# Five weight units instead of four on the first token tile at two stage changes of a two-block transformer kernel

## Chip, cores and metric

The kernel runs on one core of one Trainium2 chip. The metric is the device time of one launch in microseconds (us), lower is better; a figure without a word beside it is the median of several launches on one chip.

## What is computed

The reference is two transformer blocks in a row on one sequence of 256 tokens with model width 1024, in float32. The part that matters here is the second block:

```python
u = rms_norm(x, ffn1_norm_g) * (1 + sc1) + sh1
x = x + 0.5 * g1 * swiglu(u, ffn1_w_in, ffn1_w_out)        # D_FF_2 = 2816
u = rms_norm(x, mix_norm_g) * (1 + sc2) + sh2
z = u @ w_mix + b_mix                                      # then mLSTM and forgetting attention
...
merged = sigmoid(g_a) * (y_a @ w_branch_a) + sigmoid(g_b) * (y_b @ w_branch_b)
x = x + g2 * (merged @ w_out)
u = rms_norm(x, ffn2_norm_g) * (1 + sc3) + sh3
x = x + 0.5 * g3 * swiglu(u, ffn2_w_in, ffn2_w_out)
```

Each `rms_norm` needs the whole row of the new x, and each product after it needs the normed row: these are the points at which the chain of matmuls could break.

## The kernel before

**Units and halves.** All large products stream their weights from HBM in units: two blocks of 128 rows by 512 columns, 512 KB. The units are numbered in the order in which they are used (0 to the end). A unit's life has four steps, on four engines:

- SyncE starts its load into one of four `raw` buffers. The load of unit u+4 is issued when step "lo" of unit u is done.
- ScalarE, step `("hi", u)`: copies `raw` into a `whi` buffer, rounded (L1445).
- VectorE, step `("lo", u)`: `wlo = raw - whi` (L1807).
- TensorE, step `("half", u, t)`, once for each of the two token tiles t of 128 tokens: per block of 128 rows three matmuls, whi by the high part of the activations (L1140), wlo by the high part (L1141), whi by the low part (L1142). So a half is six matmuls and a unit is two halves.

There are five pairs of `whi`/`wlo` buffers of the kernel's own (`NW = 5`), used in rotation: unit u may be written once the unit five places earlier in the rotation has had both halves. At the start of certain stages the first three units of the new stage have lent buffers beside these (`LENT = 3`), in space that the stage before has left.

**The order.** A planner written in Python (`plan`) makes one list, `order`, before anything is built. Every engine's program goes through this list from front to back and emits its own part of each entry. So the order on each engine is fixed, and an instruction that waits holds back all that stands behind it on its engine. `half` first calls `advance`, which puts in the "hi" of every unit that `may_prep` allows and that lies at or below `at["limit"]`, or is the unit about to be used. `hold(n)` sets this limit to n units beyond the last one put in, `hold(0)` allows no further one, and `hold(None)` lifts it. A "lo" follows its "hi" after `LO[...]` further halves (1 for the product with `w_out_2`, 2 for the first feed-forward's last product, 2 for the second feed-forward's first), or at once when its unit is next.

**A change of stage.** `tail` takes the last units of the old stage (`todo`), first all of them on token tile 0, then all on tile 1. While tile 1 is multiplied, x of tile 0 goes through its chain:

- `resid`: bank times gate (L1885), added to x (L1889), on VectorE, then the sum of squares (L1451) on ScalarE;
- `scale`: mean (L1823), reciprocal root on GpSimd (L2391), x times the root into `W1`, half on VectorE (L1831), half on ScalarE (L1461);
- `turn`: eight transposes on TensorE (L1168) in two groups, scaled and shifted by ScalarE (L1478);
- `split`: high and low parts `hTh`, `hTl`, on VectorE (L1842, L1844).

`turn` of tile 0 stands ahead of the tile-1 half with index `LAG[stage, "turn0"]` in `todo`, which is 3 at both changes. Then `head` puts the first units of the new stage (`first`, four of them) on tile 0, with `turn` of tile 1 after the one with index `LAG[stage, "turn1"]` (1 for "mix", 2 for "ffn2"), and at last all four on tile 1.

**The two changes in numbers of units.** Into the mixer ("mix"): `todo` is 159 to 162, the last four units of the first feed-forward's second output block `ffn1o1`; `first` is 163 to 166 (`conv0`, of which 163 to 165 have lent buffers and 166 has the buffer that 158 had); 167 is the small `gate` unit (288 columns in its buffer), 168 to 171 are `conv1`. The limit after `scale` is `hold(4)`. Into the second feed-forward ("ffn2"): `todo` is 248 to 251 (`wob0`, `wob1`); ahead of them 247 is the last unit of `woa1`, whose bank is the one that 250 and 251 complete; `first` is 252 to 255 (`ffn2a0`, of which 252 to 254 have lent buffers and 255 has the buffer that 247 had); 256 to 259 are `ffn2b0`. The limit after `scale` is `hold(0)`.

The lines of the first of these changes in the list `order`, as they stand before, with "hi" and "lo" (tile in the last place of a half):

```
half 158 0, half 158 1, mods, hi 163, 164, 165, 166, lo 162, half 159 0, half 160 0, lo 163..166,
half 161 0, half 162 0, resid 0, scale 0, half 159 1, hi 167, half 160 1, hi 168, half 161 1, turn 0, split,
lo 167, half 162 1, resid 1, split, scale 1, lo 168, half 163 0, half 164 0, turn 1, split, ...
```

Of the kernel before, what the change touches and what calls it, by code (L numbers as in the profile page):

```python
# [13 lines left out]
LEAD = 4  # L14
# [2 lines left out]
NEVER = (None, 0)  # L17


LAG = {("attn", "behind0"): 2, ("attn", "between0"): 0, ("attn", "between1"): 1, ("attn", "first"): 3,  # L20
       ("attn", "hold1"): 0, ("attn", "turn1"): 0, ("attn_a", "wait"): 21, ("attn_as", "round"): 21,
       ("attn_as", "wait"): 1, ("attn_as", 0): 4, ("attn_as", 1): 14, ("attn_as", 2): 23, ("attn_as", 3): 11,
       ("attn_at", "round"): 24, ("attn_at", 0): 7, ("attn_at", 1): 1, ("attn_at", 2): 3, ("attn_at", 3): 9,
# [116 lines left out]
def build(nc, d, out):  # L140
# [208 lines left out]
    blocks, units, order = {}, [], []  # L349
# [69 lines left out]
    def plan():  # L419
# [4 lines left out]
        def lag(name, i, n=1):  # L424
            return LAG.get((name, i), n)

# [11 lines left out]
        def tick(most=3):  # L438
            for j in jobs:
                j[1] -= 1  # L440
            for j in list(jobs):
                if most and j in jobs and j[1] <= 0:
                    advance_job(j)
                    most -= 1

        def drain(*names):
            while any(j[2] in names or not names for j in jobs):
                tick(99)

        def drain_of(names):  # L450
            while any(j[2] in names for j in jobs):
                tick(99)
# [18 lines left out]
        def hold(more):  # L471
            at["limit"] = len(units) - 1 if more is None else at["prep"] - 1 + more
# [3 lines left out]
        def half(u, t):  # L476
            at["act"] = blocks[units[u][0]]["act"]
            for w in lows:
                w[1] -= 1
            advance(u)  # L480
            assert at["prep"] > u
            order.append(("half", u, t))
            if t:
                assert u == at["done"]
                at["done"] += 1
            at["tick"] += 1
            every = ADA[blocks[units[u][0]]["act"]]
            if every and at["tick"] % every == 0 and not at["quiet"]:
                ada_step()
# [4 lines left out]
        def ada_until(j):  # L494
            while ("ada", j) not in done:
                next(at["ada"])

        def gemm(key, skip=0, leave=0):
            b = blocks[key]
            if b["pair"] == key and not skip:  # L500
                while None not in pairs.held:
                    tick()
                pairs.take(key)
            for u in b["units"][skip:len(b["units"]) - leave]:
                for t in range(2):
                    half(u, t)
                    tick()
# [10 lines left out]
        def split(stage, t, p):  # L518
            order.append(("split", stage, t, p))

        def turn(stage, t, between=0, behind=None, late=False):
            for p in range(2):
                misc.take("norm", stage, t, p)
                misc.drop("norm", stage, t, p)
                sqr.take("n", stage, t, p)
                sqr.drop("n", stage, t, p)
                order.append(("turn", stage, t, p))
                if not (p and late):
                    split(stage, t, p)
                hold(behind if p else between)  # L530
                advance()
# [166 lines left out]
        def resid(stage, key, c, gate, t):  # L698
            if gate:
                nat.take("res", stage, t, c)  # L700
                nat.drop("res", stage, t, c)
            if stage != "end":
                sqr.take("x", stage, t, c)
                sqr.drop("x", stage, t, c)
            order.append(("resid", stage, key, c, gate, t))
# [3 lines left out]
        def head(stage, then):  # L709
            first = blocks[then]["units"][:LAG["attn", "first"] if stage == "attn" else LEAD]  # L710
            assert LAG[stage, "turn1"] < len(first)
            pairs.take(then)
            hold(lag(stage, "hold1", 0))
            for i, u in enumerate(first):
                half(u, 0)
                tick()
                if i == LAG[stage, "turn1"]:
                    turn(stage, 1, lag(stage, "between1", 0))
            for u in first:
                half(u, 1)  # L720
                tick()
            if stage == "attn":
                sums("attn")
                for t in range(2):
                    order.append(("scale", "attn", t))
                order.append(("setup", "rope"))
            at["quiet"] = False

        def tail(stage, ends, then, gate, *second):
            todo = [u for key, n, _ in ends for u in blocks[key]["units"][-n:]]  # L730
            late = lag(stage, "late", 1)
            at["quiet"] = True
            opened.add(then)
            for u in todo:
                half(u, 0)
                tick()
            for key, _, c in ends:
                resid(stage, key, c, gate, 0)
            if then:
                order.append(("scale", stage, 0))  # L740
                hold(lag(stage, "hold0", 1))
            drain_of(second)
            for i, u in enumerate(todo):
                if then and i == LAG[stage, "turn0"]:
                    turn(stage, 0, lag(stage, "between0", 0), 0, late)
                half(u, 1)
                tick()
            for key, _, c in ends:
                resid(stage, key, c, gate, 1)
                pairs.drop(blocks[key]["pair"])  # L750
            if then:
                if late:
                    split(stage, 0, 1)
                order.append(("scale", stage, 1))
                head(stage, then)

        def residual(prefix, stage, then=None, gate=False):
            gemm(f"{prefix}0")
            for t in range(2):
                resid(stage, f"{prefix}0", 0, gate, t)  # L760
            pairs.drop(f"{prefix}0")
            gemm(f"{prefix}1", leave=LEAD)
            if stage in FFN:
                ada_until(6 * FFN[stage] + 3)
                order.append(("mods", stage))
            tail(stage, [(f"{prefix}1", LEAD, 1)], then, gate)

        at["ada"] = ada()
        hold(0)
        turn("attn", 0, LAG["attn", "between0"], LAG["attn", "behind0"])  # L770
        head("attn", "qa")
# [22 lines left out]
        drain("attn_b", "sub0")  # L794
        ada_step()
        tail("mlp", [("ob0", 2, 0), ("ob1", 2, 1)], "up0", False, "sub1")

        def job_u(name):
# [7 lines left out]
        for c in range(8):  # L806
            gemm(f"up{c}", skip=0 if c else LEAD)
            add(f"up{c}", job_u(f"up{c}"))
            tick()
        residual("down", "ffn1", "ffn1a0")  # L810

        def job_glu(name, b, n):
# [6 lines left out]
        def ffn(m, last_gate, stage, then=None):  # L819
            for i, (c0, n) in enumerate(HB):  # L820
                gemm(f"{m}a{i}", skip=0 if i else LEAD)
                for _ in natural(f"{m}g{i}"):
                    tick()
                order.append(("silu", m, i))
                pairs.drop(f"{m}a{i}")
                gemm(f"{m}b{i}")
                add(f"{m}g{i}", job_glu(f"{m}g{i}", f"{m}b{i}", n))
                tick()
            ada_until(last_gate)
            residual(f"{m}o", stage, then, gate=True)  # L830
# [185 lines left out]
        nat.drop("sig", 1)  # L1016
        drain("mT0")
        gemm("woa0")
        gemm("woa1")
        drain()  # L1020
        ada_until(11)
        ada_until(6 * FFN["ffn2"] + 3)
        order.append(("mods", "ffn2"))
        tail("ffn2", [("wob0", 2, 0), ("wob1", 2, 1)], "ffn2a0", True)
        ffn("ffn2", 17, "end")
        assert at["done"] == len(units)

    plan()


# [1658 lines left out]
```

## Time and profile before

| what | value |
|---|---|
| median of 3 launches | 1002.22 us |
| lowest and highest | 1001.82, 1003.26 us |
| profiled execution, its own time | 1003.34 us |
| profiled execution, its span (first to last instruction) | 1002.0 us |
| mean granted TensorE clock over the span | 0.997 of full speed |
| TensorE busy | 976.3 us (97%) |
| VectorE, ScalarE busy | 719.2 us, 527.7 us |

All times inside the kernel below are us from the start of the span. The profiled execution took 1.3 us more than its span, and 1.1 us more than the median.

### The profile page before, as it was taken

What the parts mean: (1) busy time and instruction counts of PE and PEld (TensorE: products, weight loads), DVE (VectorE), ACT (ScalarE), POOL (GpSimd) and SP (SyncE); (2) the same over time, 40 slices, a digit from 0 to 9 for tenths busy, and PEclk for the clock granted to TensorE, in tenths of its full rate; (3) what the DMA queues carried; (4) which work ended last, traced back from release to release, by engine and by line L of the source; (5) the groups of instructions that cost most, each with busy time, mean ns of one, the idle gap of its engine ahead of it and who ended that gap; (6) DMA issues with size and microseconds to landing.
All of it is one profiled execution on the core that took longest, in us unless ns stands there. A gap on an engine that the chain in (4) does not pass through costs nothing.

```text
span 1002.0 us, 12880 instructions
## 1 busy us (share of the span) xinstructions
PE 976.3 (97%) x4772; PEld 805.3 (80%) x4772; DVE 719.2 (72%) x1073; ACT 527.7 (53%) x811; POOL 57.4 (6%) x62
## 2 busy tenths in 40 slices
PE   8997999999999999999989999999999989999998
PEld 6876788888788888888878788877888868888886
DVE  5966778888776767777759978677658766566653
ACT  6675654554436444444457845467565474443531
POOL 3310100000000000000000022021000000000000
PEclk9998999999999999999999999999999999999999
DMA  7930648888885888688745766875555727754861
GB/s 250 295 126 1 229 154 269 273 280 263 286 286 186 267 266 263 203 274 304 249 135 190 251 179 191 260 254 167 174 177 204 229 103 242 238 189 137 271 205 49
DMA packets 116428, 214.64 MB, mean 214 GB/s; under 512 B 9042, under 2 KB 16490, under 8 KB 116110
## 3 DMA queue, kind: packets, MB, share of 16 engines
q1 hardware_dynamic: 116222, 213.73, 65.5%
q8 instruction: 38, 0.62, 0.2%
q14 instruction: 24, 0.20, 0.1%
q10 hardware_dynamic: 144, 0.10, 0.0%
HBM read 212.71 MB, written 2.13 MB: 214 GB/s over the span
## 4 chain that ended last, share of the span: by engine, by line
PE 88%; DVE 6%; ACT 2%; DMA 2%; issue 1%; POOL 0%; SPq 0%; ACTq 0%; DVEq 0%
PE ps L1140 26%; PE ps L1142 26%; PE ps L1141 26%; PE ps L1190 3%; DVE wlo L1807 2%; PE ps L1232 2%; PE ps L1277 1%; DMA raw<-in_w_mix 1%; PE ps L1258 1%; ACT whi L1445 1%; PE ps L1168 1%; DMA raw<-in_w_in 1%; DVE qkT L2243 1%; PE ps L1326 1%; PE ps L1328 1%
## 5 line engine op out<-in xcount | busy, mean ns | idle before, releaser
L1445 ACT ACTIVATE whi<-raw 128x1024 fp32r<-128x1024 f32 (+1 forms) x306 | 313.5, 1032 | 295.6 <-PE ps L1142 224.5
L1807 DVE TENSOR_TENSOR wlo<-raw,whi 128x1024 fp32r<-128x1024 f32 (+1 forms) x306 | 361.7, 1195 | 85.9 <-ACT whi L1445 84.6
L1140 PE MATMUL ps<-whi,hTh 128*128 128x512 f32 (+1 forms) x832 | 326.8, 393 | 3.4 <-DVE wlo L1807 3.4
L1142 PE MATMUL ps<-whi,hTl 128*128 128x512 f32 (+1 forms) x832 | 316.2, 380 | 0.0
L1141 PE MATMUL ps<-wlo,hTh 128*128 128x512 f32 (+1 forms) x832 | 316.0, 380 | 0.0
L1140 PEld LDWEIGHTS ps<-whi,hTh 128*128 128x128 f32 x832 | 156.6, 188 | 34.5 <-DVE wlo L1807 4.9
L1142 PEld LDWEIGHTS ps<-whi,hTl 128*128 128x128 f32 x832 | 156.6, 188 | 30.9
L1141 PEld LDWEIGHTS ps<-wlo,hTh 128*128 128x128 f32 x832 | 156.9, 189 | 27.1 <-issue 0.5
L2149 DVE SCALAR_TENSOR_TENSOR aacc<-araw,cs,aacc 128x512 f32<-128x512 f32 x126 | 94.3, 749 | 2.5
L2391 POOL TENSOR_TENSOR stat<-stat,mhalf 128x8 f32<-128x8 f32 (+3 forms) x29 | 36.1, 1255 | 640.4 <-DVE stat L1823 482.0
L1140 PE MATMUL ps<-whi,uh_ffn 128*128 128x512 f32 x176 | 69.3, 394 | 0.0
L1141 PE MATMUL ps<-wlo,uh_ffn 128*128 128x512 f32 x176 | 68.6, 390 | 0.0
L1142 PE MATMUL ps<-whi,ul_ffn 128*128 128x512 f32 x176 | 68.5, 389 | 0.0
L1140 PE MATMUL ps<-whi,uh 128*128 128x512 f32 x128 | 51.6, 403 | 0.0
L1142 PE MATMUL ps<-whi,ul 128*128 128x512 f32 x128 | 49.9, 390 | 0.0
L1141 PE MATMUL ps<-wlo,uh 128*128 128x512 f32 x128 | 49.9, 390 | 0.0
L1142 PEld LDWEIGHTS ps<-whi,ul_ffn 128*128 128x128 f32 x176 | 33.0, 188 | 7.0
L1140 PEld LDWEIGHTS ps<-whi,uh_ffn 128*128 128x128 f32 x176 | 33.0, 188 | 7.0 <-issue 0.2
L1141 PEld LDWEIGHTS ps<-wlo,uh_ffn 128*128 128x128 f32 x176 | 33.1, 188 | 6.8 <-issue 0.2
L1811 DVE TENSOR_TENSOR ul_ffn<-ps,uh_ffn 128x512 fp32r<-128x512 f32 x22 | 15.2, 689 | 32.3 <-ACT uh_ffn L1541 32.3
L1190 PE MATMUL ps<-ident,nat 128*128 128x128 f32 x208 | 31.0, 272 | 0.9 <-ACT P L1594 0.9
L1190 PEld LDWEIGHTS ps<-ident,nat 128*128 128x128 f32 x208 | 25.5, 140 | 7.2 <-issue 1.5
(253 smaller groups left out, 1083.6 us busy)
## 6 DMA issues: line engine op xcount, KB each, us to landing
raw<-in_ffn_w_in SPq DMA_DIRECT2D x80, 512.0 KB, 4.5
araw<-in_w_ada SPq DMA_DIRECT2D x72, 512.0 KB, 4.8
raw<-in_w_mix SPq DMA_DIRECT2D x64, 512.0 KB, 4.5
raw<-in_ffn_w_out SPq DMA_DIRECT2D x44, 512.0 KB, 4.9
raw<-in_w_up SPq DMA_DIRECT2D x32, 512.0 KB, 4.6
raw<-in_w_down SPq DMA_DIRECT2D x32, 512.0 KB, 4.7
raw<-in_w_out SPq DMA_DIRECT2D x16, 512.0 KB, 4.2
raw<-in_w_in SPq DMA_DIRECT2D x14, 512.0 KB, 5.8
```

Of the source, the lines that this page charges most:

```text
L1140: pe.e.matmul(o, ah, h[:, j, :], start=s0, stop=False, skip_group_check=True)
L1141: pe.e.matmul(o, ah, l[:, j, :], start=False, stop=False, skip_group_check=True)
L1142: r = pe.e.matmul(o, al, h[:, j, :], start=False, stop=s1, skip_group_check=True)
L1168: r = pe.e.transpose(bank[:, c * 128:(c + 1) * 128], src[:, (4 * p + c) * 128:(4 * p + c + 1) * 128], ident[:, :])
L1190: r = pe.e.transpose(bank[:, c * 256 + t * 128:c * 256 + t * 128 + 128], src[t][:, (2 * p + c) * 128:(2 * p + c + 1) * 128], ident[:, :])
L1232: return pe.e.matmul(bank[:, c * w:(c + 1) * w], Q[rows, hp + c, ts], K[rows, kc(c), 0:w], start=True, stop=True)
L1258: r = pe.e.transpose(bank[:, c * 128:(c + 1) * 128], buf[:, c * 128:(c + 1) * 128], ident[:, :])
L1445: act.e.activation(uflat(whi, u), uflat(raw, u), ACT.Copy).then_inc(hi.up(u), 1)
L1807: v.tensor_tensor(uflat(wlo, u), uflat(raw, u), uflat(whi, u).bitcast(f32), SUB).then_inc(lo_dve.up(u), 1)
L1811: v.tensor_tensor(o, bank, h.bitcast(f32), SUB).then_inc(lower.up(name, p), 1)
L2149: r = v.scalar_tensor_tensor(acc[:, :], buf[:, k, :], cs[:, kt:kt + 1], acc[:, :], MUL, ADD)
L2391: g.tensor_tensor(o, a, mhalf[:, 0:n], ALU.pow).then_inc(rstd.up(*key), 1)
```

## The change

The number of units that go through token tile 0 ahead of tile 1 is made a setting of the stage (`"lead"`), 5 for "mix" and 4 for the others that use `residual`. At the change into the second feed-forward, where `todo` was two units of each of two blocks, the last unit of `woa1` is put ahead of these four, so that `todo` has five as well. `turn0`, `turn1`, `hold0`, the five buffers and the four units of `first` stay as they are.

```diff
-LAG = {("attn", "behind0"): 2, ("attn", "between0"): 0, ("attn", "between1"): 1, ("attn", "first"): 3,
+LAG = {("mix", "lead"): 5, ("end", "lead"): 4, ("ffn1", "lead"): 4, ("attn", "behind0"): 2, ("attn", "between0"): 0, ("attn", "between1"): 1, ("attn", "first"): 3,
...
-        def tail(stage, ends, then, gate, *second):
-            todo = [u for key, n, _ in ends for u in blocks[key]["units"][-n:]]
+        def tail(stage, ends, then, gate, *second, more=()):
+            todo = [*more, *(u for key, n, _ in ends for u in blocks[key]["units"][-n:])]
...
-            gemm(f"{prefix}1", leave=LEAD)
+            lead = lag(stage, "lead", LEAD)
+            gemm(f"{prefix}1", leave=lead)
...
-            tail(stage, [(f"{prefix}1", LEAD, 1)], then, gate)
+            tail(stage, [(f"{prefix}1", lead, 1)], then, gate)
...
-        gemm("woa1")
+        gemm("woa1", leave=1)
...
-        tail("ffn2", [("wob0", 2, 0), ("wob1", 2, 1)], "ffn2a0", True)
+        tail("ffn2", [("wob0", 2, 0), ("wob1", 2, 1)], "ffn2a0", True, more=blocks["woa1"]["units"][-1:])
```

## Rows read from the trace of the kernel before

**Rows 1.** The page: busy time, share of the span and instructions of each engine.

```profile
PE 976.3 (97%) x4772; PEld 805.3 (80%) x4772; DVE 719.2 (72%) x1073; ACT 527.7 (53%) x811; POOL 57.4 (6%) x62
```

**Rows 2.** TensorE's waits over the span: us in total, times, longest.

```profile
PE ps L1168 <- DVE W L1831: 4.3, 4, 1.7
```

**Rows 3.** Timeline of TensorE, change into the mixer: start, duration, instruction, [idle before].

```profile
493.28 0.39 PE L1140 MATMUL ps<-whi,uh_ffn 128*128 128x512 f32 x1
...
501.44 0.39 PE L1140 MATMUL ps<-whi,uh_ffn 128*128 128x512 f32 x1
...
506.62 1.07 PE L1168 MATMUL ps<-ident,W 128*128 128x128 f32 x8 [0.94 <-DVE W L1831]
...
509.61 0.47 PE L1140 MATMUL ps<-lent_hi,hTh 128*128 128x512 f32 x1 [0.53 <-DVE hTl L1844]
...
514.34 1.06 PE L1168 MATMUL ps<-ident,W 128*128 128x128 f32 x8 [1.75 <-DVE W L1831]
```

**Rows 4.** Timeline of VectorE at the same change.

```profile
499.41 1.23 DVE L1807 TENSOR_TENSOR lent_lo<-raw,lent_hi 128x1024 fp32r<-128x1024 f32 x1 [1.28 <-ACT lent_hi L1445]
501.77 1.22 DVE L1807 TENSOR_TENSOR wlo<-raw,whi 128x1024 fp32r<-128x1024 f32 x1 [1.13 <-ACT whi L1445]
502.91 0.68 DVE L1885 TENSOR_TENSOR nat<-ps,gate 128x512 f32<-128x512 f32 x1
...
510.08 0.45 DVE L1807 TENSOR_TENSOR wlo<-raw,whi 128x288 fp32r<-128x288 f32 x1
510.45 0.68 DVE L1885 TENSOR_TENSOR nat<-ps,gate 128x512 f32<-128x512 f32 x1
```

**Rows 5.** Timeline of TensorE, change into the second feed-forward.

```profile
791.39 0.39 PE L1140 MATMUL ps<-whi,hTh 128*128 128x512 f32 x1
...
804.92 1.09 PE L1168 MATMUL ps<-ident,W 128*128 128x128 f32 x8 [1.12 <-DVE W L1831]
...
811.81 0.47 PE L1140 MATMUL ps<-lent_hi,hTh 128*128 128x512 f32 x1 [1.43 <-DVE hTl L1844]
...
813.95 1.09 PE L1168 MATMUL ps<-ident,W 128*128 128x128 f32 x8 [0.53 <-DVE W L1831]
814.79 0.48 PE L1140 MATMUL ps<-whi,hTh 128*128 128x512 f32 x1
...
816.38 0.47 PE L1140 MATMUL ps<-lent_hi,hTh 128*128 128x512 f32 x1
```

**Rows 6.** Timeline of VectorE at this change.

```profile
793.96 3.63 DVE L1807 TENSOR_TENSOR lent_lo<-raw,lent_hi 128x1024 fp32r<-128x1024 f32 x3
798.82 1.23 DVE L1807 TENSOR_TENSOR wlo<-raw,whi 128x1024 fp32r<-128x1024 f32 x1 [1.23 <-ACT whi L1445]
799.96 0.68 DVE L1885 TENSOR_TENSOR nat<-ps,gate 128x512 f32<-128x512 f32 x1
...
818.64 4.62 DVE L1807 TENSOR_TENSOR wlo<-raw,whi 128x1024 fp32r<-128x1024 f32 x4
```

**Rows 7.** Timeline of ScalarE at this change.

```profile
797.73 1.06 ACT L1445 ACTIVATE whi<-raw 128x1024 fp32r<-128x1024 f32 x1 [1.39 <-DMA raw<-in_ffn_w_in]
...
817.39 3.94 ACT L1445 ACTIVATE whi<-raw 128x1024 fp32r<-128x1024 f32 x4
```

**Rows 8.** Stretches of TensorE: from:to, length, busy (instructions), granted clock, DMA share, GB/s.

```profile
82.04:85.46 3.42, 1.80 (x16) 1.00 0.00 0
85.46:88.87 3.41, 3.21 (x14) 0.50 0.00 0
...
95.70:99.11 3.41, 3.41 (x19) 0.50 0.00 0
...
512.12:515.53 3.41, 1.66 (x13) 1.00 0.38 139
```

**Rows 9.** Timeline of TensorE: four transposes in a half-clock stretch, and four after it.

```profile
96.71 1.06 PE L1311 MATMUL ps<-ident,W 128*128 128x128 f32 x4
...
100.09 0.60 PE L1311 MATMUL ps<-ident,W 128*128 128x128 f32 x4
```

## The prediction

> **What bounds the kernel now.** I read the page first, then TensorE's waits, then the timelines of the two changes that the edit touches, and at last the granted clock. TensorE is busy for 976.3 of 1002.0 us [rows 1], so the whole kernel is one stream of matmuls, and the time moves only where that stream stops. Over the span the transposes of `turn` wait four times for VectorE's `W1`, 4.3 us in all, 1.7 at most [rows 2]; all four are at the two changes touched here. That is what is on offer.
>
> The unit of account is a half, written unit/tile. From the start of 158/0 at 493.28 to that of 159/1 at 501.44 lie six halves (158/0, 158/1, 159/0 to 162/0): 8.16 us, 1.36 us each [rows 3].
>
> *Into the mixer, before.* The three tile-1 halves end at 501.44 + 3 x 1.36 = 505.5; the transposes start at 506.62, 1.1 late. The next stage's first half waits again until 509.61, and the transposes of tile 1 start only at 514.34, after 1.9 us of silence [rows 3]. The start of the chain is not TensorE's: half 162/0 was over at 501.6, but `resid` began at 502.91, directly behind "lo" of unit 166, which had itself waited for ScalarE [rows 4].
>
> *Into the second feed-forward, before.* From 791.39 nine halves take TensorE to 803.6; the transposes start at 804.92. The third half of the new stage waits until 811.81, the transposes of tile 1 until 813.95; then 255/0 starts at 814.79 and 252/1 at 816.38 [rows 5]. Here too `resid` starts at 799.96 behind a "lo", that of unit 255 [rows 6], whose "hi" had waited 1.39 us for its load [rows 7].
>
> **What the change moves.** No matmul, copy or load is added or dropped; places in the list change. I went through the planner's rules.
>
> *First edit, mixer.* The five units 158 to 162 now hold all five buffers during tile 0. Unit 166, which needs the buffer of 158, can therefore get its "hi" only after half 158/1. So "lo 166" leaves its place ahead of `resid`. `turn0` is 3 as before, so three tile-1 halves still stand ahead of the transposes, and two behind them instead of one.
> - Chain of tile 0: the "lo" of 165 starts at 499.41; back-to-back ones in a run of four cost 4.62/4 = 1.16 us each [rows 4, 6]. `resid` starts at 500.57. Its operand is ready: five halves from 493.28 end at 500.1. It starts 502.91 - 500.57 = 2.34 us earlier, and with it the transposes, at 504.28. TensorE gets there after eight halves, at 504.2: that wait goes.
> - Then two halves cover the way to `hTl`, which was ready 3.0 us after the transposes began (506.62 to 509.61). Transposes 0.84 [rows 5] and two halves, 2.72, are 3.6 us: the second wait goes too.
> - But "lo 166" now stands between `split` and `resid` of tile 1, ahead of the small "lo" of the gate unit at 510.08 [rows 4]. VectorE reaches `resid` of tile 1 by 2.34 - 1.16 = 1.18 us earlier, at 509.27 and not 510.45. Half 162/1 is over at 504.28 + 3.56 = 507.8, so VectorE sets this start, and the transposes of tile 1 come at 513.16.
> - TensorE will be there at 507.84 + 2.72 = 510.6 and wait 2.6 us. At this point exactly the same halves are done as before at 514.34. What counts is this one number: **the mixer part saves 1.2 us**; most of what is taken from the first two waits is given back in the third.
> - Moved with it: "hi 168" goes behind the tile-1 `turn`, so three of them follow there, not two, and "lo 168" behind the last `split`. Load 170, which SyncE issues behind "lo 166", and load 172, behind "lo 168", start some 6 and 4 us later; units 170 and 172 are used at least 10 us after that. Cost nothing; without this cover each would cost what it is late, and the bound that I keep is 0 to 1.2, the whole gain.
>
> *Second edit, second feed-forward, up to the tile-1 transposes.* The units 247 to 251 hold the five buffers, so 255 (buffer of 247) is not prepared during tile 0, and `resid` follows directly behind the last of the lent ones. The three from 793.96 on end at 797.59 [rows 6]; `resid` starts at 797.55 and not 799.96, 2.4 us earlier. Its operands are ready (five halves from 791.39 end at 798.2, and the second bank is wanted at 798.9). Nothing else enters this chain, since no "lo" stands between the splits here. Transposes of tile 0 at 802.5 (TensorE is there after eight halves, at 802.3), third half of the new stage at 809.4, transposes of tile 1 at **811.5, 2.4 us earlier**.
>
> *Second edit, behind them.* Here is the price. The limit set after `scale` is `hold(0)`: no unit beyond 254 may be prepared until `turn` of tile 1 lifts it. Before, 255 had been prepared ahead of that; now it has not (the mixer has `hold(4)`, so its 166 passes). "hi 255" therefore stands on ScalarE behind the tile-1 scaling, where before a run of four "hi" began at 817.39 [rows 7], and "lo 255" on VectorE behind the last `split`, where the run of four "lo" began at 818.64 [rows 6]. TensorE's next entry is half 255/0, and 252/1 to 254/1, which could run, stand behind it.
> - With the 2.4 us: "hi 255" at 815.0, "lo 255" at 816.2 to 817.5, half 255/0 at 817.6.
> - TensorE is free at 811.5 + 0.84 = 812.4: it stands still for **5.2 us**.
> - 252/1 starts at 817.6 + 1.4 = 819.0 and not 816.38 [rows 5]: **this edit costs 2.6 us net**.
> - Behind it: four "lo" (256 to 259) follow within 5 us, and their units are wanted from 819.0 + 4 x 1.36 = 824.4 on; load 259 is issued behind "lo 255", at 817.5 where it was 800.0, and is wanted at 832. Nothing.
>
> **The clock.** Twice the granted clock fell from 1.00 to 0.50, that is from 2.4 to 1.2 GHz: at 85.46, after attention matmuls with long gaps (1.80 us busy of 3.42), and at 95.70; it stayed low for 3.41 us each time. The stretch from 512.12 with only 1.66 us busy, dense 512-column work around a gap of 1.9 us, stayed at 1.00 [rows 8]. A silence of 5.2 us is nearly three times that, and I take it that the clock falls. Four transposes took 1.06 us at the low level and 0.60 at the high one [rows 9]: 43% of low-clock time is lost. One such stretch wholly over matmuls costs 3.41 x 0.43 = 1.5 us. The bounds: 0 (it does not fall, or falls and recovers within the silence) and 2.9 (two in a row). I take **1.5**. The Trainium skill, "TensorE: Matmul & The Clock Gate", section "Part 1: The HAM clock gate (the "warmup" mystery)", has the throttled clock as the default state that activity releases, which speaks against any edit that lets the array fall silent; by its rule the sum holds the 1.5, by the 1.9-us gap alone it would not.
>
> **Sum.** -1.2 + 2.6 + 1.5 = **+2.9 us**. On the profiled execution's own 1003.34 that is 1006.2; that execution lay 1.1 above the median of 1002.22, and the forecast for a median is 1005.1. About 0.2%, 2.0 us, is what a measurement of this kernel can tell from no change, so 1000.2 and 1004.2 are the bounds of "same".
>
> **Rivals and chances.**
> - *The forecast*, 1005.1: 0.52. Its own range, with the clock's cost from 0.6 to 2.4, is 1004.2 to 1006.0.
> - *The clock holds.* For it: the 1.9-us gap left no mark. Then -1.2 + 2.6 = +1.4, 1003.6: 0.20.
> - *The stall swallows more: the mixer saves nothing*, because a late load or "lo" behind it (load 172 above all) takes the 1.2 back. +2.6 + 1.5 = +4.1, 1006.3: 0.12. Against it: ten us of slack.
> - *The clock falls in the mixer's gap as well*, which grows from 1.9 to 2.6 us: +2.9 + 1.5 = +4.4, 1006.6: 0.09.
> - *Other side: unit 255 is ready in time*, if some entry that I overlooked prepares it ahead of the tile-1 `turn`. Then the 2.4 us stay: -1.2 - 2.4 = -3.6, 998.6: 0.07. It decides at "lo 255": with its end at 812.4 the whole 3.6 is kept, each us later costs one, and even without the clock the change only pays if it ends before 816.1. Against it: `hold(0)` and the buffer rule leave no entry.
>
> Faster by over 0.2%: the last case, 0.08 with rounding. Within: the clock case and the low end of the forecast, 0.30. Slower: 0.62. The range 1002.6 to 1007.2 takes in all but the last case and the tails, some 0.15 together.
>
> **What would show it.** In the profile after: (1) mixer, `resid` of tile 0 directly behind the third "lo" on lent buffers, tile-1 transposes with about 2.6 us idle before them, and 1.2 us earlier than 514.34; (2) second feed-forward, tile-0 transposes with next to no wait, tile-1 transposes 2.4 us earlier against the start of this change; (3) one L1140 matmul there with about 5 us idle before it, released by L1807, which did not exist before; a run of five "hi", not four; (4) the granted clock at 0.50 for a stretch that starts in or just behind this silence. The prediction is wrong if (3) is absent or short, and 1.5 us too high if (4) is absent.

## The result and the profile after

The changed kernel took 1006.27 us (median of 10 launches, 1003.66 to 1007.67) against 1001.76 (10 launches, 1000.46 to 1005.14) for the kernel before on the same chip: ratio 1.0039, 95% interval 1.0028 to 1.0051, so 2.8 to 5.1 us slower. In a second comparison it was 1.0036 (1.0024 to 1.0048). The forecast was 2.9 us slower.

The profiled execution has a span of 1002.3 us and took 1003.66, the lowest of its ten; so spans are not compared here, but stretches between the same two points of work. TensorE in the profile after, at the change into the mixer (L1169 is the transposes' line, L1141 that of the first matmul; both moved down by one line):

```profile
491.23 0.39 PE L1141 MATMUL ps<-whi,uh_ffn 128*128 128x512 f32 x1
...
502.12 1.07 PE L1169 MATMUL ps<-ident,W 128*128 128x128 f32 x8
...
505.79 0.39 PE L1141 MATMUL ps<-lent_hi,hTh 128*128 128x512 f32 x1
...
510.99 1.06 PE L1169 MATMUL ps<-ident,W 128*128 128x128 f32 x8 [2.31 <-DVE W L1832]
```

The first row is the start of 158/0. The waits before the tile-0 transposes and before the new stage's first half are gone, and the one before the tile-1 transposes has grown, to 2.3 us. From the first row to the last are 19.76 us, against 514.34 - 493.28 = 21.06 before [rows 3]: 1.3 us saved. VectorE at the same place:

```profile
497.26 1.23 DVE L1808 TENSOR_TENSOR lent_lo<-raw,lent_hi 128x1024 fp32r<-128x1024 f32 x1 [1.19 <-ACT lent_hi L1446]
498.41 0.68 DVE L1886 TENSOR_TENSOR nat<-ps,gate 128x512 f32<-128x512 f32 x1
...
505.59 1.58 DVE L1808 TENSOR_TENSOR wlo<-raw,whi 128x1024 fp32r<-128x1024 f32 x2
507.09 0.69 DVE L1886 TENSOR_TENSOR nat<-ps,gate 128x512 f32<-128x512 f32 x1
```

The residual of tile 0 follows the third "lo" on lent buffers directly, without the one that stood between them in [rows 4]; that one now stands, with the gate unit's, ahead of the residual of tile 1.

TensorE at the change into the second feed-forward, the counterpart of [rows 5] (the first row is the start of 247/0):

```profile
787.36 0.39 PE L1141 MATMUL ps<-whi,hTh 128*128 128x512 f32 x1
...
805.30 0.47 PE L1141 MATMUL ps<-lent_hi,hTh 128*128 128x512 f32 x1 [0.31 <-DVE hTl L1845]
...
807.44 1.09 PE L1169 MATMUL ps<-ident,W 128*128 128x128 f32 x8 [0.51 <-DVE W L1832]
813.41 0.79 PE L1141 MATMUL ps<-whi,hTh 128*128 128x512 f32 x1 [4.88 <-DVE wlo L1808]
814.00 0.63 PE L1142 MATMUL ps<-wlo,hTh 128*128 128x512 f32 x1
...
817.41 0.48 PE L1141 MATMUL ps<-lent_hi,hTh 128*128 128x512 f32 x1
817.73 0.40 PE L1142 MATMUL ps<-lent_lo,hTh 128*128 128x512 f32 x1
```

The tile-1 transposes come 20.08 us after 247/0 and not 22.56: 2.5 us gained. Then half 255/0 waits 4.88 us for its "lo". Its matmuls and the first three of the next half take 0.63 us each, where 0.39 is usual, until 817.41. What half 255/0 waited for, on VectorE and ScalarE:

```profile
812.14 4.62 DVE L1808 TENSOR_TENSOR wlo<-raw,whi 128x1024 fp32r<-128x1024 f32 x4
```

```profile
810.89 3.93 ACT L1446 ACTIVATE whi<-raw 128x1024 fp32r<-128x1024 f32 x4
816.95 1.06 ACT L1446 ACTIVATE whi<-raw 128x1024 fp32r<-128x1024 f32 x1 [2.13 <-DMA raw<-in_ffn_w_in]
```

The runs of four "lo" and "hi" begin with unit 255 now, and a fifth "hi" (259) follows when its late load has landed, before its use: no half behind 255/0 waits. The granted clock of these stretches (columns as in [rows 8]):

```profile
807.35:810.77 3.42, 1.09 (x8) 1.00 0.00 0
810.77:814.18 3.41, 0.77 (x2) 0.50 0.00 0
814.18:817.59 3.41, 3.41 (x10) 0.50 0.89 291
817.59:821.00 3.41, 3.41 (x17) 1.00 1.01 341
```

The clock falls to 1.2 GHz in the silence, stays there for 6.8 us, and 4.2 us of these lie over matmuls.

### The profile page after: what moved, and what is told of

It is laid out like the page before. It is cut to its first block, busy times and chain, and to the rows that moved or that the text cites. A ratio compares the mean times of both kernels' runs of the same rounds, so it can differ in the third digit from the quotient of the medians.

```text
span 1002.3 us, 12879 instructions
## 1 busy us (share of the span) xinstructions
PE 975.6 (97%) x4772; PEld 805.5 (80%) x4772; DVE 719.3 (72%) x1073; ACT 528.2 (53%) x811; POOL 56.5 (6%) x62
## 3 DMA queue, kind: packets, MB, share of 16 engines
HBM read 212.71 MB, written 2.13 MB: 214 GB/s over the span
## 4 chain that ended last, share of the span: by engine, by line
PE 88%; DVE 6%; ACT 2%; DMA 2%; issue 1%; SPq 1%; POOL 0%; ACTq 0%; DVEq 0%; POOLq 0%
PE ps L1141 26%; PE ps L1143 26%; PE ps L1142 26%; PE ps L1191 2%; DVE wlo L1808 2%; PE ps L1233 1%; PE ps L1278 1%; PE ps L1169 1%; DMA raw<-in_w_in 1%; PE ps L1259 1%; DMA scr_b<-scr_t 1%; DVE qkT L2244 1%; PE ps L1327 1%; PE ps L1329 1%; DMA raw<-in_w_mix 0%
## 5 line engine op out<-in xcount | busy, mean ns | idle before, releaser
L1141 PE MATMUL ps<-whi,hTh 128*128 128x512 f32 (+1 forms) x832 | 327.6, 394 | 7.3 <-DVE wlo L1808 7.3
L1141 PEld LDWEIGHTS ps<-whi,hTh 128*128 128x128 f32 x832 | 157.0, 189 | 38.3 <-DVE wlo L1808 8.6
L1141 PE MATMUL ps<-whi,uh_ffn 128*128 128x512 f32 x176 | 69.3, 394 | 0.0
L1141 PE MATMUL ps<-whi,uh 128*128 128x512 f32 x128 | 51.6, 403 | 0.0
L1141 PEld LDWEIGHTS ps<-whi,uh_ffn 128*128 128x128 f32 x176 | 33.1, 188 | 6.9 <-issue 0.2
```

The lines of the kernel that those rows point to most:

```text
L1141: pe.e.matmul(o, ah, h[:, j, :], start=s0, stop=False, skip_group_check=True)
```

## Experiments

Each kernel was timed in rounds with the kernel before on one chip. The table gives, from each kernel's one profile, the time between points of equal work: A is 158/0 to the mixer's tile-1 transposes, B is 158/0 to the first matmul of the gate product (all of unit 166 done), C is 247/0 to the tile-1 transposes, D is 247/0 to 256/0 (all of unit 255 done). Every end is the start of an instruction in the timeline. The last but one column is B + D less that of the kernel before.

| kernel | A | B | C | D | B + D less before | measured ratio (95%) |
|---|---|---|---|---|---|---|
| before | 21.06 | 30.19 | 22.56 | 30.55 | 0 | 1 |
| changed | 19.76 | 28.85 | 20.08 | 34.93 | +3.0 | 1.0039 (1.0028 to 1.0051) |
| changed, again | 20.68 | 31.38 | 20.25 | 34.79 | +5.4 | 1.0036 (1.0024 to 1.0048) |
| mixer edit alone | 19.66 | 28.75 | 22.94 | 30.91 | -1.1 | 0.9995 (0.9984 to 1.0007) |
| second edit alone | 20.83 | 29.96 | 20.23 | 35.07 | +4.3 | 1.0041 (1.0025 to 1.0058) |
| limit one | 19.62 | 30.32 | 20.64 | 28.62 | -1.8 | 0.9972 (0.9957 to 0.9987) |
| limit one at both | 19.22 | 28.35 | 20.80 | 28.76 | -3.6 | 0.9959 (0.9945 to 0.9974) |
| 255/0 behind | 20.09 | 30.78 | 20.37 | 31.28 | +1.3 | 0.9992 (0.9978 to 1.0005) |
| four units, late "lo" | 20.79 | 29.91 | 21.71 | 29.71 | -1.1 | 0.9989 (0.9976 to 1.0002) |
| silence filled | 19.94 | 29.03 | 20.08 | 32.98 | +1.3 | 1.0032 (1.0018 to 1.0047) |
| both filled | 20.28 | 29.37 | 20.15 | 33.05 | +1.7 | 1.0015 (1.0003 to 1.0028) |
| limit one, mixer filled | 19.96 | 29.05 | 20.84 | 28.83 | -2.9 | 0.9975 (0.9964 to 0.9987) |

One profile is one execution; the ratio is over several. The same piece of work differs between profiles: the unaltered changed kernel has 19.76 and 20.68 us for A, and the second change, when it is as before, has 30.55 and 30.91 us for D. For A the rows show why. The last "hi" on a lent buffer, that of unit 165, waits for its load, and the whole chain of tile 0 hangs on it. The first row is from the profile after, the second from "changed, again":

```profile
496.17 1.06 ACT L1446 ACTIVATE lent_hi<-raw 128x1024 fp32r<-128x1024 f32 x1 [1.43 <-DMA raw<-in_w_mix]
...
496.86 1.06 ACT L1446 ACTIVATE lent_hi<-raw 128x1024 fp32r<-128x1024 f32 x1 [2.22 <-DMA raw<-in_w_mix]
```

That is 4.94 and 5.86 us after 158/0. In all eight profiles with five units and the mixer's limit of 4 this "hi" starts 4.81 to 5.86 us after 158/0, and the tile-1 transposes come 14.81 to 14.83 us behind it. Their A averages 20.0, against 20.9 in the three profiles with four units: 0.9 us saved on average, 0.1 to 1.4 by the pair chosen. No run shows why the load lands at different times.

**The mixer edit alone.** The second edit undone:

```diff
-        gemm("woa1", leave=1)
+        gemm("woa1")
...
-        tail("ffn2", [("wob0", 2, 0), ("wob1", 2, 1)], "ffn2a0", True, more=blocks["woa1"]["units"][-1:])
+        tail("ffn2", [("wob0", 2, 0), ("wob1", 2, 1)], "ffn2a0", True)
```

> Only the mixer edit: five units there, four at the change into the second feed-forward as in the kernel before. Theory: the transposes of tile 1 come 1.2 to 1.3 us earlier, counted from the start of half 158/0, with about 2.5 us of idle before them; the change into the second feed-forward is as before (22.6 us from 247/0 to the tile-1 transposes). Against the kernel before -1.2 to -1.3 us, about 1000.5, which the times alone can hardly tell from no change. Rival, the mixer saves nothing because units 170 to 172 come late: a wait for a 'lo' behind the change, and 0 or more.

A is 1.4 us shorter and B 1.4: the gain is kept up to the gate product, and no wait for a "lo" appears. In the times it is not told from zero: 11 launches had a median of 1001.69 against 1002.31.

**The second edit alone.**

```diff
-LAG = {("mix", "lead"): 5, ...
+LAG = {("mix", "lead"): 4, ...
```

> Only the edit at the change into the second feed-forward; the mixer as in the kernel before. Theory (late unit 255 plus low clock): tile-1 transposes 2.4 us earlier, then about 5 us of silence, then one or two stretches at half clock; +2.4 net for the wait and +1 to +2.9 for the clock, together about +4.3 us against the kernel before. Rival 1 (the clock costs nothing in the usual run): +2.4. Rival 2 (the loss is in the mixer): 0.

4.3 us by the profile, 2.5 to 5.8 by the times. The loss is at the change into the second feed-forward; the first edit by itself costs nothing that can be seen.

**The late unit: the limit lifted by one.** Both edits, and

```diff
-       ("ffn2", "hold0"): 0, ...
+       ("ffn2", "hold0"): 1, ...
```

> The changed kernel, both edits in, with hold0 of the second feed-forward 1 in place of 0, so that unit 255 is prepared as soon as half 247/1 has freed its buffer. Theory (the loss is unit 255's late preparation and the silence it makes): no silence before 255/0, clock at 1.00 throughout, the 2.4 us gained ahead of the tile-1 transposes stay but for some 0.3 us by which 'hi 255' on ScalarE delays the scaling of tile 0: -2.1 there and -1.3 in the mixer, -3.4 against the kernel before, about 998.3. Rival (the loss comes from five units holding all five buffers as such, by later loads and copies): still slower than before, with waits for 'lo' moved to units 256 to 259.

This settles where the loss came from: one number in the planner's table turns 4 us of loss into 2.8 (1.3 to 4.3) of gain, median 999.24 against 1002.31, with all five buffers held as in the changed kernel. The 3.4 us that were expected lie within the interval. TensorE there, from 247/0 at 788.25 on:

```profile
806.75 0.47 PE L1141 MATMUL ps<-lent_hi,hTh 128*128 128x512 f32 x1 [1.01 <-DVE hTl L1845]
...
808.89 1.09 PE L1169 MATMUL ps<-ident,W 128*128 128x128 f32 x8 [0.54 <-DVE W L1832]
809.74 0.47 PE L1141 MATMUL ps<-whi,hTh 128*128 128x512 f32 x1
```

255/0 follows the transposes at once. C is 0.56 us longer than in the changed kernel, since "hi 255" stands on ScalarE ahead of the scaling and shifting of tile 0's transposes (0.3 expected). But the profile also shows what the expectation had not: the clock fell in the *mixer*, behind the silence before the tile-1 transposes.

```profile
508.04:511.45 3.41, 1.21 (x10) 1.00 0.75 282
511.45:514.86 3.41, 3.41 (x9) 0.50 0.00 0
```

B less A is 10.70 us in this execution and 9.09 in the first profile of the changed kernel: one low stretch over matmuls costs 1.6 us.

**The clock: unread work in the silence.** The changed kernel, and on TensorE ahead of half 255/0:

```diff
+            if u == blocks["ffn2a0"]["units"][-1] and t == 0:
+                w = uview(whi, u - 1)
+                for _ in range(18):
+                    pe.e.matmul(ps[7][:, 0:512], hTh[:, 0, 0:128], w[:, 0, :], start=True, stop=True)
```

> The changed kernel with 18 further 512-column matmuls on TensorE into a bank that nothing uses then, between the tile-1 transposes and half 255/0, i.e. inside the silence: 18 x 0.227 = 4.1 us of work in 5 us of waiting. They write nothing that is read, and unit 255 is as late as in the changed kernel. Theory (the low clock is the second part of the loss): clock stays at 1.00 there, half 255/0 starts at the same place, and the kernel is about 1.9 us faster than the changed one, some +1.1 against the kernel before. Rival (the clock costs nothing): same time as the changed kernel, +3 to +4.5.

```profile
810.05 1.09 PE L1173 MATMUL ps<-ident,W 128*128 128x128 f32 x8 [0.51 <-DVE W L1836]
810.89 4.38 PE L1132 MATMUL ps<-lent_hi,hTh 128*128 128x512 f32 x18
816.02 0.50 PE L1145 MATMUL ps<-whi,hTh 128*128 128x512 f32 x1 [0.74 <-DVE wlo L1812]
```

```profile
810.05:816.02 5.97, 5.23 (x26) 1.00 0.00 0
```

255/0 starts 26.05 us after 247/0 (789.97), the same as in the changed kernel (813.41 - 787.36 = 26.05), the clock stays at 1.00, and D is 1.95 us shorter, as the theory has it. The times did not show it: 1005.67, with launches from 1002.3 to 1009.4, against an expected 1003.4 or so. The launches' own mean granted clock has a median of 0.993, no higher than in the changed kernel (0.993), so it was low elsewhere in many of them; where, their records do not say. I therefore filled the mixer's silence too, with nine such matmuls, and ran the unaltered changed kernel beside it.

> The changed kernel with both silences filled with unread matmuls: 18 ahead of half 255/0, as in the earlier run, and 9 in the 2.6 us before the mixer's tile-1 transposes. Theory (low clock in either silence is part of the loss): clock at 1.00 at both changes in every execution; against the unaltered changed kernel on the same chip -1.9 us from the one and up to 0.8 from the other (a fall in perhaps half of the executions, 1.6 us each), -2 to -3 together. Rival (the filling takes from the engines beside TensorE, or the clock costs less in executions without the profiler): -0.5 or nothing.

> The changed kernel itself, unaltered, on the same chip in the same rounds, as what the filled one is to be compared with. Every theory expects the first result again: about +4 us against the kernel before, and in the profile a stretch at half clock at the silence ahead of half 255/0.

1003.27 against 1005.99, 2.7 us less, with intervals (+0.3 to +2.8 and +2.4 to +4.8 us against the kernel before) that overlap only a little. The launches' mean granted clock agrees: its median is 0.993 in both sets of the changed kernel, 0.996 to 0.997 in the three sets of the kernel before, and 0.9965 with both silences filled; 6.8 us at half clock take 0.0034 off the mean of such a span. So the low clock is a part of the loss in ordinary launches too, though how much of the 2.7 us belongs to which silence the times do not show. The profile of the unaltered one has both falls:

```profile
508.85:512.26 3.41, 1.11 (x9) 1.00 0.82 296
512.26:515.68 3.42, 3.42 (x12) 0.50 0.00 0
...
809.22:812.63 3.41, 1.34 (x10) 1.00 0.00 0
812.63:816.05 3.42, 0.07 (x1) 0.50 0.00 0
816.05:819.46 3.41, 3.41 (x8) 0.50 0.66 194
```

**The mixer's silence filled, with the limit of one.** The same nine matmuls ahead of the mixer's tile-1 transposes:

> The kernel with both edits and hold0 of the second feed-forward 1, and 9 further 512-column matmuls on TensorE (2.0 us) into an unused bank in the silence of 2.6 us before the mixer's tile-1 transposes. Theory (that silence lets the clock fall in some executions, which took 1.6 us in the one profiled): the clock stays at 1.00 in the mixer in every execution, from the tile-1 transposes to the gate product are 9.1 us, and the times are lower than without the filling by some share of 1.6 us. Rival (the clock falls there too seldom to matter): the same times, or 0.1 us above by the filling's own cost.

The clock stayed at 1.00 at both changes and B less A is 9.09 us. The median, 999.57, is no lower than without the filling (999.24, in another comparison); the gain of some share of 1.6 us, less the filling's own cost, is not seen in these times. Inconclusive.

**The order on TensorE.** The changed kernel with half 255/0 put off:

```diff
             for i, u in enumerate(first):
+                if stage == "ffn2" and i == 3:
+                    continue
                 half(u, 0)
...
             for u in first:
+                if stage == "ffn2" and u == first[-1]:
+                    half(u, 0)
+                    tick()
                 half(u, 1)
```

> The changed kernel with half 255/0 put behind half 254/1, so that unit 255 is as late as in the changed kernel, but TensorE's next entry after the tile-1 transposes is 252/1, which needs only the split of tile 1. Theory (it is the order on TensorE that turns a late unit into a silence): no wait for 'lo 255'; 1.6 us idle before 252/1 in place of 4.9; 255/0 starts about when its 'lo' is long done; ahead of unit 256 the change into the second feed-forward is 1.1 us shorter than in the kernel before (29.4 us from 247/0, against 30.55), and with the mixer's 1.3 the kernel is some 2.4 us below the kernel before. Rival (late copies and the late load 259 cost by themselves): a wait moves to 255/0 or to 256 to 259, and the time stays above the kernel before.

```profile
809.80 1.09 PE L1174 MATMUL ps<-ident,W 128*128 128x128 f32 x8 [0.53 <-DVE W L1837]
812.23 0.76 PE L1146 MATMUL ps<-lent_hi,hTh 128*128 128x512 f32 x1 [1.34 <-DVE hTl L1850]
```

Unit 255 is as late as in the changed kernel, and nothing waits for its "lo": its half starts at 817.99 without idle time. 4.7 us are gone in the times (from a ratio of 1.0039 to 0.9992). So the lateness by itself made nothing wait; it cost because TensorE's fixed order had this half next. The kernel is 0.8 us (interval -2.2 to +0.5) and not 2.4 below the kernel before, and its profile says why D is 31.28 and not 29.4: the clock fell here as well, from 812.17 to 815.58, after the silence of 1.3 us that follows those before the third half and before the transposes.

**Four units with a late "lo".** The kernel before, with

```diff
+            if stage == "ffn2":
+                at["limit"] = blocks[then]["units"][2]
...
-       ("ffn2", "hold0"): 0, ...
+       ("ffn2", "hold0"): 1, ...
```

> The kernel before, four units at both changes, but at the change into the second feed-forward unit 255 may be prepared only behind the residual of tile 0 (its 'hi' ahead of half 248/1, its 'lo' ahead of 249/1). Theory: the residual starts 2.4 us earlier as with five units, but TensorE reaches the transposes of tile 0 only after its nine halves, so they come 1.3 us earlier (12.25 us from 247/0 and not 13.53), and all behind them too: -1.3 us against the kernel before. Five units with the same limit gained 1.9 us there; so two thirds of the gain need no fifth unit. Rival (the fifth unit is what gains): no change against the kernel before.

TensorE reaches the tile-0 transposes 12.24 us after 247/0 and finds them ready, as expected; D is 0.84 us shorter than before, not 1.3, since "lo 255" stands ahead of the first split, and the new stage's first half waits 0.54 us for `hTl`:

```profile
806.92 1.23 DVE L1809 TENSOR_TENSOR wlo<-raw,whi 128x1024 fp32r<-128x1024 f32 x1 [1.22 <-ACT whi L1447]
808.06 0.29 DVE L1844 CAST hTh<-sq 128x256 fp32r<-128x256 f32 x1
```

The ratio, 0.9989, does not exclude no change. With five units and this limit D is 1.93 us shorter. So by these profiles a good two fifths come from moving a "lo" out of the way of the residual and not two thirds, the rest from the fifth unit; against the other profile of this change as before (D 30.91) it is about half.

**The best of them: the limit of one at both changes.**

```diff
-       ("ffn2", "hold0"): 0, ...
+       ("ffn2", "hold0"): 1, ...
...
-       ... ("mix", "hold0"): 4,
+       ... ("mix", "hold0"): 1,
```

> As the run with hold0 of the second feed-forward 1, and hold0 of the mixer 1 in place of 4, so that only unit 166 and not the small gate unit 167 is prepared between the halves of tile 1. Theory: ScalarE scales tile 0 of the mixer 0.3 us earlier (no 'hi 167' ahead of it) and VectorE reaches the residual of tile 1 another 0.37 us earlier (no 'lo 167' ahead of it), so the tile-1 transposes come 0.7 us earlier than with hold0 4, at 19.0 us from the start of half 158/0 against 19.7, and the silence before them is 1.9 us and not 2.6. Time: 0.7 us below the kernel with only the first of these limits, about 998.5. Rival (that start is set by something else, a transfer or ScalarE's later work): 19.7 as before and the same time.

```profile
506.17 1.22 DVE L1808 TENSOR_TENSOR wlo<-raw,whi 128x1024 fp32r<-128x1024 f32 x1
507.30 0.68 DVE L1886 TENSOR_TENSOR nat<-ps,gate 128x512 f32<-128x512 f32 x1
```

```profile
511.19 1.07 PE L1169 MATMUL ps<-ident,W 128*128 128x128 f32 x8 [1.59 <-DVE W L1832]
```

The gate unit's "lo" no longer stands between unit 166's and the residual. The tile-1 transposes come 14.11 us after "hi 165" starts and not 14.82: the 0.7 us that was expected. A is 19.22 us (19.0 expected, but this load landed later), the silence 1.6 us, and the kernel takes 997.97 us against 1001.80: ratio 0.9959 (0.9945 to 0.9974), 4.1 us faster than the kernel before and some 8 faster than the changed one. That the second limit gains beyond the first (0.9959 against 0.9972) the times alone do not show, since the intervals overlap.

## Why the prediction was right

**Mixer, -1.2 us.** In the profile after -1.3, in the way foreseen: two waits gone, most of it given back in the third, because VectorE has "lo 166" ahead of the residual of tile 1. That the size fits so well is partly luck: the prediction takes the start of "lo 165" from one profile, and it moves with a load, so that the saving is 0.4 us in the second profile of the same kernel and 0.9 on average. The third wait is 2.2 to 2.3 us by the profile, which has 1.75 for what the prediction calls 1.9 and foresees as 2.6. The loads that start later cost nothing: B less A is 9.09 us here and 9.13 before.

**Second feed-forward up to the tile-1 transposes, -2.4.** Measured -2.5 (C 20.08). The run with the second edit alone has 20.23, the second profile of the changed kernel 20.25.

**The wait behind them, 5.2 us, +2.6 net.** In the profile 4.88 us of idle by the modelled ends of the matmuls. The foreseen run of five "hi" came as four and a fifth that waited 2.13 us for its load, which cost nothing. 255/0 starts 26.05 us after 247/0, where it was 814.79 - 791.39 = 23.40 before [rows 5]. With the silence filled, so that the clock is out of it, D is +2.4. The limit of one and the half put off show from two sides that this is the cause: the "lo" is late because `hold(0)` keeps unit 255 back, and the lateness counts because its half is next on TensorE.

**The clock, +1.5.** The mechanism was right and the size low, for two reasons: more low-clock time over matmuls, and a second place. At the second feed-forward the low clock stood for 6.8 us, two stretches, in all three profiles of kernels with this silence unfilled (the changed one twice, and the second edit alone), and cost 34.93 - 32.98 = 1.95 us. In the profile after, 4.2 us of it lay over matmuls, more than the one full stretch that the term was made of, and at 0.43 us between starts and not 0.23 they lose 47% of it, a little more than the 43% read from four transposes. The Trainium skill, "TensorE: Matmul & The Clock Gate", section "Part 1: The HAM clock gate (the "warmup" mystery)", has the throttled clock as the default and activity as what releases it. The trace agrees: matmuls ran from 813.41, and the granted clock was back at 1.00 from 817.59.

**The rival of the mixer's gap, given 0.09, is in part true.** The clock fell there in three of the six profiles in which this silence is 2.2 to 2.3 us and unfilled (limit one, 255/0 behind, changed again), and in none of the four in which it is 1.6 to 1.75 us (before, second edit alone, four units, limit one at both), and in neither of those in which it was filled. At 1.6 us each that is 0.8 us on average, if the profiles stand for the launches. It would take back most of the 0.9 us that the edit saves on average. That fits the mixer edit alone, which saves 1.4 us in its profile, where the clock held, and 0.5 in its times; but the interval there holds 1.4 us of gain and 0.6 of loss, so the times do not show it.

Summed anew, after the fact: -0.9 + 0.8 at the mixer, +2.4 + 1.95 at the second feed-forward, +4.2 us (with the 1.3 of the profile after it is +3.9); measured +3.9 and +3.6. The median of 1006.27 lies within the stated range and 1.2 us above the forecast. The times by themselves (2.8 to 5.1) would also fit the rivals of +4.1 and +4.4; it is the profiles that choose, for the mixer saved time and its clock fell in a part of them. They exclude +1.4 and -3.6.

What stays open: the share of ordinary launches in which the clock falls in the mixer's gap, which could be read only from profiles, and what makes the load of unit 165 land early or late.

## What to carry to other kernels

A stage change that holds one more buffer also holds back whatever was to be written into it. Look for the next unit that needs that buffer, for the rule or queue position that lets it be prepared, and for the place of its use in the order of the engine that consumes it; a setting that was harmless with one buffer free (here a limit of 0) can become the longest wait. When an idle gap is moved rather than removed, compare its new length with those that the clock has survived in several traces, not in one: here 1.6 to 1.75 us left it up in four profiles, and 1.3 us behind two shorter waits did not. And before a saving is read from one profile, look at what its chain starts from; if that is a load, take the time from the load's landing on.

## What the runs showed of the hardware

TensorE's granted clock fell to 0.50 after silences much shorter than I had expected: 2.2 to 2.3 us, and once 1.3 us where two waits of 0.3 and 0.5 us lay ahead. At the low level 512-column matmuls start every 0.427 us, against 0.227. The same wait does not always do it: 2.2 to 2.3 us before the same transposes left the clock at 1.00 in three of six profiles. In the attention phase the mean clock from 78 to 103 us ranged from 0.73 to 1.00 between profiles whose work there is the same. Half 158/0 starts at 490.5 to 491.4 us in the four with 1.00, and at 495.3 and 495.4 in the two with 0.73. Much of the spread of the times of the kernel before, 999.3 to 1006.3, goes with the clock too: its 12 launches with a mean granted clock of 0.993 or less average 1005.1 us, its 30 with 0.998 or more 1000.8. No run changed the attention phase, so that it is the cause is not shown.
